# Feed-forward output by seven half-size products in a decoder trunk on one Trainium2 core

## The reference

```python
def swiglu(h, w_in, w_out):
    gate, up = jnp.split(h @ w_in, 2, axis=-1)
    return (jax.nn.silu(gate) * up) @ w_out        # w_out: 2816 x 1024
x = x + 0.5 * swiglu(rmsnorm(x, norm), w_in, w_out)
```

## Time and profile before

| | |
|---|---|
| median of 3 runs | 1964.09 us (1963.82 to 1964.57) |
| profiled execution, first to last instruction (span) | 1962.7 us |
| what lies around the span, against the median | 1.4 us |
| TensorE busy | 1943.1 us (99%) |
| VectorE, ScalarE, GpSimd busy | 75%, 45%, 11% |
| moved by DMA | 189.5 MB, mean 97 GB/s |

### The profile page before, as it was taken

One profiled execution on the slowest core, in us unless ns is written; L12 is line 12 of the kernel. 1 busy time (PEld: TensorE's weight loads), 2 busy tenths in 40 slices (PEclk: granted clock), 3 DMA queues, 4 the chain that ended last, 5 costly groups with the idle time before them and its releaser, 6 DMA issues.

```text
span 1962.7 us, 23707 instructions
## 1 busy us (share of the span) xinstructions
PE 1943.1 (99%) x9192; PEld 1617.8 (82%) x9192; DVE 1466.0 (75%) x1855; ACT 892.6 (45%) x1245; POOL 222.1 (11%) x166
## 2 busy tenths in 40 slices
PE   9999999999999999999999999999999999999998
PEld 7888888888888888888888888888897898888886
DVE  8999944886767859999843999983368779989722
ACT  6555632352434435555621555562168445554510
POOL 0000012000000031000021000002146440000121
PEclk9999999999999999999999999999999999999999
DMA  5233132331313320422232242223222014222331
GB/s 173 86 141 117 60 103 90 130 134 43 135 43 134 126 90 10 155 94 86 89 104 85 99 155 93 86 89 104 85 85 86 1 60 156 86 86 101 104 101 60
DMA packets 76189, 189.53 MB, mean 97 GB/s; under 512 B 4144, under 2 KB 12336, under 8 KB 73008
## 3 DMA queue, kind: packets, MB, share of 16 engines
q1 hardware_dynamic: 76080, 188.04, 27.5%
HBM read 185.92 MB, written 2.10 MB: 96 GB/s over the span
## 4 chain that ended last, share of the span: by engine, by line
PE 90%; DVE 6%; issue 2%; ACT 1%; POOL 1%; DMA 0%; SPq 0%; DVEq 0%; ACTq 0%; POOLq 0%
PE bank L2464 13%; PE bank L2466 13%; PE bank L2465 13%; PE bank L2456 12%; PE bank L2458 12%; PE bank L2457 12%; PE bank L2683 3%; PE bank L2685 3%; PE bank L2684 3%; PE bank L2564 2%; DVE part_lo L1566 1%; PE bank L2694 1%; PE bank L2944 1%; PE bank L2883 1%; DVE gated_lo L1830 1%
## 5 line engine op out<-in xcount | busy, mean ns | idle before, releaser
L1025 ACT ACTIVATE part_hi<-quad_w 128x1024 fp32r<-128x1024 f32 x280 | 293.1, 1064 | 278.1 <-PE bank L2466 195.2
L1566 DVE TENSOR_TENSOR part_lo<-quad_w,part_hi 128x1024 fp32r<-128x1024 f32 x280 | 329.7, 1216 | 23.3 <-ACT part_hi L1025 22.9
L2456 PE MATMUL bank<-gated_hi,out_hi 128*128 128x512 f32 x704 | 274.7, 390 | 0.0
L2458 PE MATMUL bank<-gated_hi,out_lo 128*128 128x512 f32 x704 | 273.9, 389 | 0.0
L2457 PE MATMUL bank<-gated_lo,out_hi 128*128 128x512 f32 x704 | 273.9, 389 | 0.0
L2464 PE MATMUL bank<-part_hi,s_hi 128*128 128x512 f32 x640 | 252.3, 394 | 0.6 <-DVE part_lo L1566 0.6
L2466 PE MATMUL bank<-part_hi,s_lo 128*128 128x512 f32 x640 | 249.4, 390 | 0.0
L2465 PE MATMUL bank<-part_lo,s_hi 128*128 128x512 f32 x640 | 249.1, 389 | 0.0
L2464 PE MATMUL bank<-part_hi,xn_hi 128*128 128x512 f32 x608 | 238.0, 391 | 1.9 <-DVE part_lo L1566 1.9
L2465 PE MATMUL bank<-part_lo,xn_hi 128*128 128x512 f32 x608 | 237.3, 390 | 0.0
L2466 PE MATMUL bank<-part_hi,xn_lo 128*128 128x512 f32 x608 | 237.2, 390 | 0.0
(11 more groups left out here) (307 smaller groups left out, 3539.3 us busy)
## 6 DMA issues: line engine op xcount, KB each, us to landing
quad_w<-w_ffn_in SPq DMA_DIRECT2D x80, 1024.0 KB, 7.4
out_raw<-w_ffn_out SPq DMA_DIRECT2D x64, 704.0 KB, 4.2
quad_w<-w_ret_in SPq DMA_DIRECT2D x14, 1024.0 KB, 7.3
rest_raw<-w_ffn_in SPq DMA_DIRECT2D x32, 256.0 KB, 5.3
quad_w<-w_ret_in SPq DMA_DIRECT2D x16, 512.0 KB, 5.6
quad_w<-w_ret_out SPq DMA_DIRECT2D x8, 1024.0 KB, 5.3
w_raw<-w_dsa SPq DMA_DIRECT2D x7, 1024.0 KB, 5.0
x_res<-x_in SPq DMA_DIRECT2D x8, 256.0 KB, 6.3
```

Source lines behind the costliest of these rows:

```text
L1025: nc.scalar.activation(in_four(part_hi[part_slot(h)]), source, copy).then_inc(part_hi_made, 1)
L1566: nc.vector.tensor_tensor(in_four(part_lo[part_slot(h)]), source, in_four(part_hi[part_slot(h)]).bitcast(FP32), ALU.subtract)\
L2456: mm(to, w_hi_of[:, at:at + width], hi, start=start, stop=False)
L2458: return mm(to, w_lo_of[:, at:at + width], hi, start=False, stop=stop)
```

## The change

The gated matrix X (512 tokens, 2816 features) and `w_out` are both cut in four: x11 and x12 are the first 256 tokens with the first and second 11 feature tiles, x21 and x22 the other 256 tokens; w11, w12 the upper half of `w_out` for output tiles 0 to 3 and 4 to 7, w21, w22 the lower half. Seven products of 256 tokens by 11 tiles by 4 output tiles take the place of eight: x11 w11, x12 w21, S1T1, S2T2, S3T3, x22T4, S4w22, in this order. The T are sums of quarters of `w_out`, the S sums of quarters of X.

* **TensorE**: 28 steps (product p, output tile dt), each 11 x 3 = 33 matmuls of 256 columns, 924 in all. Two output tiles share a bank. Four of the products continue in banks that already hold an earlier product.
* **Weights**: 16 loads by SyncE as before, and 16 accumulating DMAs issued by GpSimd, which add a unit in HBM to one that lies in SBUF. T1 is w11 plus w12, T2 is T1 plus w22, T4 is T2 plus w21, all made in place in `out_sum`; T3 is loaded w12 plus w22, in the unit's own place. Each unit of 28 is split by ScalarE (`out_high`) and VectorE (`out_low`). Hi and lo of a step lie in places A to F and I: `OUT_PLACES` gives the place of each step, and a place is free when the last step that used it is done.
* **Left operands**: for each of the seven products the 2816 columns (11 tiles of 256 tokens) are split in two or three pieces (`left_high`, `left_low`), and VectorE makes S1 to S4 (`sum_left`).
* **Results**: VectorE adds plus or minus half of two output tiles of a bank at a time to the residual stream (`add_out`), 14 times; an add that another product's step waits for counts on `x_added`.
* **Tail**: the last FFN adds its last product in three pieces, and ScalarE squares four tiles at the end where it squared one.

The core of the difference:

```diff
+OUT_PRODUCTS = ("x11w11", "x12w21", "S1T1", "S2T2", "S3T3", "x22T4", "S4w22")
+OUT_LOADS = {"x11w11": "w11", "x12w21": "w21", "S3T3": "w12", "S4w22": "w22"}
+OUT_ADDS = {"S1T1": "w12", "S2T2": "w22", "S3T3": "w22", "x22T4": "w21"}
+OUT_PLACES = "AIBC" + "DEAB" + "CDEA" + "BCDE" + "ABCD" + "EABC" + "FABC"
...
+    def out_before(i):
+        return max((j for j in range(i) if OUT_PLACES[j] == OUT_PLACES[i]), default=None)
...
+                for name in ("x12w21", "S3T3", "S4w22"):
+                    for dt in range(OUT_TILES):
...
+                        else:
+                            sp.wait_ge(unit_done, u0 + out_before(i) + 1)
+                        load_out_unit(name, dt)
...
+                def add_out_unit(name, dt):
+                    i = out_count(name) + dt
+                    nc.gpsimd.dma_start(out_bufs(i)[0][:, :], w_ffn_out[out_source(f, OUT_ADDS[name], dt)],
+                                        accum_op=ALU.add).then_inc(out_added[name][dt], 16)
+                for dt in range(OUT_TILES):
+                    pool.wait_ge(w_lo_made, u0 + out_count("x11w11") + dt + 1)
+                    add_out_unit("S1T1", dt)
+                for dt in range(OUT_TILES):
+                    pool.wait_ge(w_lo_made, u0 + out_count("S1T1") + dt + 1)
+                    add_out_unit("S2T2", dt)
+                for dt in range(OUT_TILES):
+                    pool.wait_ge(out_loaded["S3T3"][dt], loads_count(f, "S3T3"))
+                    add_out_unit("S3T3", dt)
+                    pool.wait_ge(w_lo_made, u0 + out_count("S2T2") + dt + 1)
+                    add_out_unit("x22T4", dt)
...
+                for p in range(2, N_PRODUCTS - 1):
+                    i = OUT_TILES * p
+                    left_high(p, 0)
+                    out_high(i)
+                    left_high(p, 1)
+                    out_high(i + 1)
+                    out_high(i + 2)
+                    out_high(i + 3)
...
+                left_low(4, 0)
+                out_low(16)
+                left_low(4, 1)
+                out_low(17)
+                sum_left("S4")
+                add_out("x12", 3, two[0], "P6", -0.5)
+                out_low(18)
+                out_low(19)
+                add_out("x12", 3, two[1], "P6", -0.5)
...
+                def out_step(i):
...
+                    elif name == "S2T2":
+                        pe.wait_ge(x_added, x_added_count(s, f"x11 P1 {ab}"))
+                    elif name == "S3T3":
+                        pe.wait_ge(x_added, x_added_count(s, f"x12 P6 {ab}"))
+                    elif name == "x22T4":
+                        pe.wait_ge(x_added, x_added_count(s, f"x22 P7 {ab}"))
...
+                    pe.wait_ge(w_lo_made, u0 + i + 1)
+                    to = cols(bank[n], first, HALF_SEQ)
...
+                    for k in range(HALF_TILES):
...
+                        mm(to, w_hi_k, left_hi_k, start=first_in, stop=False, skip_group_check=joins)
+                        mm(to, w_hi_k, left_lo_k, start=False, stop=False, skip_group_check=joins)
+                        done = mm(to, w_lo_k, left_hi_k, start=False, stop=last_in, skip_group_check=joins)
+                    done.then_inc(unit_done, 1)
```

More of the change, by code:

```diff
@@ new lines, in out_source, with loads_count, adds_count, out_count @@
+    def out_source(f, quarter, dt):
+        half, columns = {"w11": (0, 0), "w12": (0, 1), "w21": (1, 0), "w22": (1, 1)}[quarter]
+        return f * FFN_OUT_UNITS + 2 * (OUT_TILES * columns + dt) + half
+    def loads_count(f, name):
+        return 16 * (2 * f + (1 if name in ("x11w11", "x12w21") else 2))
+    def adds_count(f, name):
+        return 16 * (f + 1 if name == "S3T3" else 3 * f + ("S1T1", "S2T2", "x22T4").index(name) + 1)
+    def out_count(name):
+        return OUT_PRODUCTS.index(name) * OUT_TILES
@@ new lines, in left_count, with left_tiles, gated_tiles, left_raw @@
+    def left_count(f, p, j=-1):
+        return LEFTS * f + sum(len(b) for b in LEFT_BATCHES[:p]) + j + 1
+    def left_tiles(t, p, j):
+        a, b = LEFT_BATCHES[p][j]
+        return t[:, :].rearrange("p (n t) -> p n t", n=HALF_TILES)[:, a:b]
+    def gated_tiles(t, half, tokens, a=0, b=HALF_TILES):
+        tiles = t[:, :].rearrange("p (n t) -> p n t", n=FF_TILES)
+        return tiles[:, HALF_TILES * half + a:HALF_TILES * half + b, HALF_SEQ * tokens:HALF_SEQ * (tokens + 1)]
+    def left_raw(p, j):
+        name = OUT_PRODUCTS[p]
+        if name in ("S1T1", "S2T2"):
+            return left_tiles(left_sum, p, j)
+        half, tokens = {"x11w11": (0, 0), "x12w21": (1, 0), "S3T3": (0, 0), "x22T4": (1, 1), "S4w22": (1, 0)}[name]
+        return gated_tiles(gated_raw, half, tokens, *LEFT_BATCHES[p][j])
@@ L528, in ffn_of, with x_adds, x_added_count @@
+    def x_adds(s):
+        return [n for n in X_ADDS if "P5" not in n][:4] + [f"x22 P5 {a}" for a, _ in pieces(s, "Z")] + X_ADDS[6:]
+    def x_added_count(s, name):
+        return len(X_ADDS) * ffn_of(s) + x_adds(s).index(name) + 1
     def ffn_of(s):
@@ L1250, in _ @@
+                out_high(5)
+                left_high(1, 0)
+                left_high(1, 1)
                 store_turned(GROUPS - 1, 1)
[L1251 to L1272 removed]
@@ L1905, in _ @@
                     if end:
-                        split_unit(u0)
+                        for j in range(3):
+                            left_low(0, j)
+                        out_low(0)
                     up_1(g)
@@ new lines, in _ @@
+                for i in range(OUT_STEPS):
+                    if s == len(SUBLAYERS) - 1 and i == OUT_STEPS - 1:
+                        final = ("norm", len(SUBLAYERS))
+                        pe.wait_ge(squares_done, squares_before(final) + square_ops(final))
+                        for b in range(BLOCKS):
+                            done = mm(bank[STAT_BANK][:, b:b + 1], tile(square_sum, b), ones[:, :1],
+                                      start=True, stop=True)
+                        done.then_inc(stat_done, 1)
+                    out_step(i)
+                    if i in (0, 2):
+                        turn(GROUPS - 1, i // 2)
```

533 lines of the change are left out of this document (333 added, 200 removed).

## The result

| | before | changed |
|---|---|---|
| median of 4 runs each | 1964.33 us (1963.82 to 1966.79) | 2033.64 us (2032.69 to 2035.58) |
| profiled execution, span | 1962.7 us | 2032.4 us |
| TensorE busy | 99% | 95% |

The ratio is 1.0352 (95% interval 1.0339 to 1.0365): 69 us slower. The forecast was slower by 20 us. The time lies just inside the range of 1942 to 2035 us, and only because that range was made wide enough for most of rival 1. The mechanism of the chain was named rightly and its size was not, and a third of the loss lies where I had put nothing.

The account below looks back on a forecast made before the run. TensorE alone was taken to bound the FFN output. Per FFN, -8.9 + 11.7 + 0.6 + 1.7 = +5.1 us, four times +20.4, gave 1984.5 us against 1964.09; range 1942 to 2035, the forecast's own 1972 to 1998.

Parts of the forecast that it names:

- rival 1: Accumulating DMAs cost twice a load: S3T3's chain 18.3 us late, 2010.9 us in all; chance 0.29 including beyond.
- TensorE's own work: Matmuls in each FFN output: 119.7 us removed, 110.8 us added, a gain of 8.9 us.
- VectorE's sum: VectorE's work in each FFN output: 100.5 us beside TensorE's 110.8, so it fits with 10 us to spare.
- Rival 4: VectorE bounds the FFN output, its subtractions 2.08 us beside GpSimd's squares: 1938.9 us; chance 0.20 together with rival 3.
- The chain in S3T3: Steps 16 and 18 wait for additions behind queued accumulating DMAs: 11.7 us late for each FFN.
- c = 1.5: In S3T3's DMA queue, an accumulating DMA was taken to move for 1.5 times a load's 1.9 us.
- GpSimd's issue: Issuing a DMA from GpSimd was taken as 0.6 us dearer than SyncE's 0.33: +0.6 us for each FFN.
- The clock: TensorE's granted clock dips after the stall in S3T3: +1.7 us for each FFN.
- the second wait: Step 18 waits for an addition behind step 19's subtraction: 2.0 of the 11.7 us lateness.
- The other edges: Later last tiles, GpSimd's squares and the tail at the output's end are nearly all covered: 0 plus or minus 1 us.
- rival 2: Accumulating DMAs cost as much as a load: S3T3's chain 6.8 us late, 1964.9 us, no change; chance 0.12.
- rival 3: S3T3's loads and sums run without queueing, 3.5 us late: 1942.5 us, faster; chance 0.20 together with Rival 4.

Follow-up runs that it names:

- r4: r2 with ScalarE squaring the residual stream's tiles in the FFN outputs and GpSimd only adding them up: 1938.1 us.
- r1: The changed kernel with x22T4 ahead of S3T3, T3 summed in T4's tile once split, and S3T3 in banks of its own: 1965.6 us.
- r2: r1 with VectorE's order behind the last output unit changed, the addition of the first two x12 tiles coming first: 1960.8 us.
- e1: The changed kernel with GpSimd's sixteen DMAs per FFN as plain copies, without the addition: 1993.8 us.
- e6: The changed kernel with 50 filler matmuls of the identity on TensorE ahead of step 16: 2037.3 us.
- e2: The changed kernel without the four accumulating DMAs per FFN that make T3, so S3T3 multiplies by w12 alone: 1989.2 us.

## Why the prediction was right and wrong

* **TensorE's own work, -8.9 us for each FFN: right within 1 us.** Where nothing stalls, in r4, the output parts are 8.0 us shorter than before (485.8 less 453.9, over four). The 99 matmuls from 286.91 to 298.67 of the changed kernel stand 120.0 ns apart, as the earlier trace rows had it.
* **VectorE's sum, 10 us to spare: right** inside the output part of the changed kernel. The only waits there that are VectorE's own are 0.4 to 0.8 us ahead of step 4, in three of the four parts, within the 1 us that the forecast allowed at the front. Rival 4 isn't what happened. Its mechanism, a subtraction slowed beside squares, shows once in r1 (2.35 us) and once in r2 (1.85 us), where VectorE has 2.8 us more to do.
* **The chain in S3T3: the mechanism right, its size wrong.** The failing step is "I take c = 1.5, as three movements (two reads, one write) stand against two." Measured: 1.95. Rival 1's size is the right one; that two streams are read for one is its argument, which no run shows. Its sum (+46.8 us) comes very near the loss inside the output parts (47.6 us), and that is in part luck: per FFN it is -8.9 + 18.3 + 0.6 + 1.7 = 11.7, and the runs show -8.0 (r4), 19.3 for the chain and 0.4 for the clock. Seven sums in the queue turn an error of 0.45 x 1.9 us into 6.0 us for each FFN: the widest uncertainty stood on the steepest term, and I chose the middle where no row supported it. As no row spoke for c = 1.5 either, the weight on c = 2 should not have been below that on c = 1.5.
* **GpSimd's issue, +0.6: right as a price.** 0.99 us against 0.33 is 0.66 dearer. What it costs in time no run shows by itself.
* **The clock, +1.7: wrong to add to the second wait.** The dip is there (0.50, then 0.75), but the second wait absorbs it, as the second chain already fixes when step 18 starts. What is left is 1.5 us in the third output part, where the clock is still low in step 18: 0.4 for each FFN. Where the first wait is the only one, in e1, the dip does cost 2.1 us, and in e6 it costs 1.5 us in each of three parts.
* **"The other edges", 0 plus or minus 1 us: wrong, 23.3 us.** This is the larger surprise. I had priced "The next norm's last two tiles come some 1 us later" by when they are produced, and the squares by TensorE's cover, not by GpSimd's own pace. The steps that failed: before, GpSimd had one tile left to square at the end of an output part (about 3 us); now the last four come in two pairs, and in the changed kernel the first pair stood behind 6.6 us of VectorE's other work as well. Four tiles in a row end 12.8 us after they start, and "20 us of rest products cover them" holds only in front of an FFN, not in front of retention or the attention, whose first 24 matmuls cover 5.4 us. And while they run, VectorE, which is now also late, is slowed by them. The earlier trace rows had shown that price, 2.08 us instead of 1.62, and I used it only for rival 4.
* **Rivals.** Rival 1 was the case that happened inside the output parts, e1 is rival 2 made real. What rival 3 hoped for (a queue that does not matter) is seen only in another order of the same work: r1's output parts.

The Trainium skill ("SBUF — State Buffer", Who interferes with whom) says that a VectorE instruction with two inputs in SBUF contends with a GpSimd instruction that reads SBUF. The traces agree: beside squares the subtraction of 1408 columns took 2.46 us in r2 and 1.62 elsewhere. It also says "DMA never contends with a compute engine", which fits too: VectorE's 1.62 us are the same under a full DMA share, at 307.09 in the changed kernel.

## What to carry to other kernels

A transfer that does more than copy needs a measured price before a schedule is built on it; put one in a small run first, and if none can be had, forecast from the end that the mechanism supports and not from the middle. Seven transfers queued ahead of one that is waited for multiply an error by seven: count what is in the queue, and see whether products can be ordered so that each sum is wanted one product later than the last. And when work comes in bigger pieces at the end of a stage, follow every engine that handles those pieces one by one: a helper engine that is busy for 13% of the span held some 18 us of this program, and handing half of its work to ScalarE, busy for 48%, was worth 18 to 23 us, where VectorE's new order behind the output parts gave 1 to 5. When you take transfers out of a queue, look too at which ones move up in it (e2).

## What the runs showed of the hardware

* An accumulating DMA from HBM into SBUF of 704 KB moves for 3.72 us, a plain one issued by the same engine for 1.93; full DMA engines moved 214 to 279 GB/s with sums among the loads and 419 to 421 with plain copies (windows of e1 from 295 to 305 us). GpSimd's issue takes 0.99 us for the one and 0.54 for the other in the mean (e1 against the changed kernel).
* With TensorE kept busy for 11 us and then idle for 3.13 us the granted clock still dipped, to 0.74 between 315 and 320 us (e6).
* GpSimd's squares and sums cost twice: their own time, 12.8 us for four tiles of 512 columns, and up to 2.85 times the length for VectorE's short instructions beside them (4.76 us for four in r2, 1.67 in the changed kernel with GpSimd idle).
